# Peer memory of a two-block transformer on one core: score and output stages joined into one, coefficient table laid over the ranking and score buffers, keys turned behind score block 104, half of each group's gates applied by ScalarE

## What is computed

```python
def peer_ffn(xn, w_q, keys1, keys2, u_tab, v_tab):
    ...
    s1 = jnp.einsum('thd,kd->thk', q[:, :, 0], keys1)
    s2 = jnp.einsum('thd,kd->thk', q[:, :, 1], keys2)
    v1, i1 = lax.top_k(s1, PEER_TOPK)
    v2, i2 = lax.top_k(s2, PEER_TOPK)
    cand = (v1[..., :, None] + v2[..., None, :]).reshape(T, PEER_HEADS, PEER_TOPK * PEER_TOPK)
    ...
    top, pos = lax.top_k(cand, PEER_TOPK)
    eidx = jnp.take_along_axis(cidx, pos, axis=-1)
    g = jax.nn.softmax(top.astype(jnp.float32), axis=-1).astype(xn.dtype)
    ...
        a = jax.nn.gelu(jnp.einsum('td,thkd->thk', xc, u_tab[ec]), approximate=False)
        return jnp.einsum('thk,thkd->td', gc * a, v_tab[ec])
```

## Time and profile before

| | |
|---|---|
| median of 3 runs | 3219.14 us (3217.85 to 3222.44) |
| the profiled execution's own time | 3222.66 us |
| span from its first to its last instruction | 3220.8 us |
| granted TensorE clock, mean | 0.936 |
| PE / DVE / ACT / POOL busy, share of the span | 86% / 46% / 15% / 23% |
| bytes moved by DMA | 693.93 MB, mean 215 GB/s |

### The profile page before, as it was taken

The page is one execution under the profiler, slowest core; times in us unless marked ns, Lnnn a source line. Parts: engine busy times, 40 slices in busy tenths (PEclk is TensorE's granted clock), DMA queues, the critical chain, the costliest instruction groups (busy, mean ns, idle before and its releaser), DMA issues. The chain is left out here.

```text
span 3220.8 us, 30219 instructions
## 1 busy us (share of the span) xinstructions
PE 2779.2 (86%) x10080; PEld 1558.2 (48%) x10080; DVE 1478.4 (46%) x3007; ACT 489.8 (15%) x1015; POOL 732.9 (23%) x652
## 2 busy tenths in 40 slices
PE   6997899999997599959889989998980678888877
PEld 3445534447443433314435578887870543333333
DVE  1226200104012222232047249888679977777762
ACT  2124100001101011131137121111110310000002
POOL 0000000000000022110000004554466046766740
PEclk8997998999999699979999999999995999999998
DMA  5100251340122699941300019999999069999992
GB/s 203 50 27 28 105 192 43 134 173 37 52 79 83 268 392 396 387 187 60 111 14 1 27 60 346 413 399 354 418 415 365 38 248 413 413 414 413 413 363 85
DMA packets 133341, 693.93 MB, mean 215 GB/s; under 512 B 19571, under 2 KB 20979, under 8 KB 105587
## 3 DMA queue, kind: packets, MB, share of 16 engines
q1 hardware_dynamic: 50644, 408.32, 32.0%
q0 software_dynamic: 81792, 281.07, 22.1%
q10 hardware_dynamic: 800, 3.15, 0.3%
HBM read 701.90 MB, written 48.23 MB: 233 GB/s over the span
## 5 line engine op out<-in xcount | busy, mean ns | idle before, releaser
L428 PE MATMUL ps<-hT,wring 128*128 128x256 f32 (+1 forms) x2576 | 763.0, 458 | 30.2 <-ACT pk_g L2250 14.9
L428 PEld LDWEIGHTS ps<-hT,wring 128*128 128x128 f32 x2576 | 491.3, 191 | 296.7 <-issue 252.7
L2469 PE MATMUL ps<-pm_v_rows,pm_weighted 128*128 128x512 f32 x1024 | 465.2, 604 | 62.6 <-DVE pm_weighted L2519 44.7
L2144 POOL DMA_INDIRECT pk_ring<-in_peer_u,pk_rows x256 | 304.0, 1187 | 765.3 <-DVEq L2358 538.9
L2286 DVE CUSTOM_DVE_ANT_0 pk_ring<-pk_ring,mem_x 128x1024 f32<-128x1024 f32 x256 | 309.3, 1223 | 100.6 <-DMA pk_ring<-in_peer_u,pk_rows 87.9
L2469 PEld LDWEIGHTS ps<-pm_v_rows,pm_weighted 128*128 128x128 f32 x1024 | 186.6, 190 | 340.5 <-issue 230.4
L2437 POOL DMA_INDIRECT hT<-in_peer_v,pm_idxs x192 | 258.4, 1346 | 206.3 <-PE ps L2457 107.8
L2525 DVE SCALAR_TENSOR_TENSOR h_tok<-hT,gates,h_tok 128x1024 f32<-128x1024 f32 x192 | 244.7, 1282 | 100.4 <-DMA hT<-in_peer_v,pm_idxs 81.9
L1417 POOL COPY ex_idx<-row_token 128x1 uint32 (+1 forms) x24 | 4.4, 183 | 1222.3 <-PEq L1549 1090.3
L960 PE MATMUL ps<-wring,hT 128*128 128x512 f32 (+1 forms) x544 | 213.9, 555 | 1.2 <-PEq L376 1.2
L1604 DVE TENSOR_SCALAR hT<-ps,gain,ada 128x128 f32<-128x128 f32 x192 | 63.4, 403 | 215.9 <-PE ps L1505 215.9
(11 more groups left out here) (422 smaller groups left out, 2943.9 us busy)
## 6 DMA issues: line engine op xcount, KB each, us to landing
ex_gu<-in_experts SPq DMA_DIRECT2D x32, 2048.0 KB
pm_v_rows<-in_peer_v SPq DMA_DIRECT2D x64, 1024.0 KB
ex_dn<-in_experts SPq DMA_DIRECT2D x48, 1024.0 KB
wring<-in_w_in SPq DMA_DIRECT2D x21, 2048.0 KB, 8.9
wring<-in_peer_uT SPq DMA_DIRECT2D x21, 2048.0 KB
wring<-in_experts SPq DMA_DIRECT2D x16, 2048.0 KB
ada_w<-in_w_ada SPq DMA_DIRECT2D x12, 2048.0 KB
pk_u<-in_peer_uT SPq DMA_DIRECT2D x11, 2048.0 KB
```

The costliest lines, as they stand in the source:

```text
L428: mm = env.nc.tensor.matmul(out, w[:, k, lo:hi], rhs(k), start=(k == 0), stop=(k == KD - 1))
L2144: nc.gpsimd.indirect_dma_start(ring[:, n % RING, :], None, dram["peer_u"], bass.IndirectOffsetOnAxis(ap=rows[:, n // SLOTS, n % SLOTS:n % ...
L2469: mm = nc.tensor.matmul(env.ps[:, OUT[n], :], W[q][:, j * DS + t * P:j * DS + (t + 1) * P], vr[j // 2][:, j % 2 * D + half * WBLK:j % 2 * ...
```

## The change

Both memory stages become one function and one block, `stage_memory`.

- The table `C` (128 KiB for each partition) is laid over everything that ranking and scores need; only `coef`, `gate`, `rows` and `iota` have space of their own. `C`'s first 19 groups lie over the ranking's buffers, later ones over the score blocks, the stores' buffers and `xg`, the last one over `keyT`. The ring of the gathers is `env.wring` (8 buffers), the query weights' place, so POOL waits for the queries first.
- Score blocks of `peer_uT` are loaded in pairs (1 MiB, UBUF = 4 buffers) where it was quads (2 MiB, 3 buffers); stores of scores are 256 KiB (GBUF = 4 buffers) where they were 512 KiB (2 buffers).
- The keys are turned behind score 104. The exponential of tile 3 stands behind score 104 too (it was 70).
- EARLY = 19 of the 32 groups are built while the last 24 scores and the last dots run: one round is one group, then `beside(n)` scores on PE (one or two) and some dots on DVE. The other 13 groups follow when all scores and dots are done.
- In each group DVE multiplies only the first four tokens of B with the gate, ACT the other four.
- One list of 512 gathers; those of `peer_v` follow those of `peer_u` directly. SP's block loads of `peer_v` wait for the last group's product, since `vr` lies over A and B. The output loop is written out instead of `Fori`.

```diff
-UBUF = 3
-TABLE = (8, 36, 66)
+UBUF = 4
+GBUF = 4
+TABLE = (8, 36, 66, 104)
+EARLY = 19
...
+def beside(n):
+    at = lambda k: TABLE[3] + (PK - TABLE[3]) * k // EARLY
+    return at(n), at(n + 1)
...
+    def one_hots(n):
+        if n < EARLY:
+            return [env.hT[:, :, lo + n % 2 * P:lo + (n % 2 + 1) * P] for lo in (S, 0)]
+        return [spare[:, (lo + n % 2) * D:(lo + n % 2 + 1) * D].rearrange("p (t a) -> p t a", a=PK) for lo in (0, 2)]
...
             @block.gpsimd
...
+                for n in range(2 * GT * SLOTS):
...
                     if n >= RING:
-                        pool.wait_ge(G.used, n - RING + 1)
+                        pool.wait_ge(used, n - RING + 1)
...
             @block.sync
...
+                for t in c_t[EARLY - 1]:
+                    product_done(env, sp, t)
+                for n in range(QUADS):
+                    if n >= 2:
+                        sp.wait_ge(out_done, QUAD * (n - 1))
+                    nc.sync.dma_start(W[n % 2], dram["g_dram"][n]).then_inc(w_got[n % 2], 16)
+                    if n == 0:
+                        for t in c_t[-1]:
+                            product_done(env, sp, t)
+                    for m in (2 * n, 2 * n + 1):
...
+                        nc.sync.dma_start(vr[m % 2], v_pairs[m]).then_inc(v_got[m % 2], 16)
...
             @block.tensor
...
+                def coefficients(n):
+                    A, B = one_hots(n)
+                    pe.wait_ge(ab_done, 3 * n + 3)
+                    for half, tl in enumerate(c_t[n]):
+                        if half:
+                            pe.wait_ge(b_done, n + 1)
+                        bank_ready(env, pe, tl)
+                        for j in range(4):
+                            mm = nc.tensor.matmul(env.ps[:, tl[0], j * PK:(j + 1) * PK], A[:, 4 * half + j, :],
+                                                  B[:, 4 * half + j, :], start=True, stop=True)
...
-                table(TABLE[1], PK)
+                scores(TABLE[1], TABLE[3])
                 pe.wait_ge(gate_s, NT)
...
+                for n in range(GROUPS):
+                    coefficients(n)
+                    if n < EARLY:
+                        scores(*beside(n))
...
             @block.scalar
...
+                def coefficients(n):
+                    B = one_hots(n)[1]
+                    act.wait_ge(ab_done, 3 * n + 1)
+                    for j in range(4, GRP):
+                        ins = nc.scalar.activation(B[:, j, :], B[:, j, :], ACT.Copy, scale=keyT[:, 2, n * GRP + j:n * GRP + j + 1])
+                    ins.then_inc(b_done, 1)
...
+                    for half, tl in enumerate(c_t[n]):
+                        product_done(env, act, tl)
...
-                table(TABLE[2], TABLE[2] + 4)
+                scores(TABLE[2], TABLE[3])
                 exponentials(3)
-                table(TABLE[2] + 4, PK)
...
             @block.vector
...
+                def one_hot(n):
+                    A, B = one_hots(n)
+                    ts = slice(n * GRP, (n + 1) * GRP)
+                    if n in (0, 1):
+                        for tl in key_t:
+                            evacuated(env, ve, tl)
+                    elif n == EARLY:
+                        product_done(env, ve, u_t[-1])
+                    else:
+                        product_done(env, ve, c_t[n - 2][1])
...
+                    V.tensor_tensor(B[:, 0:4, :], B[:, 0:4, :], keyT[:, 2, n * GRP:n * GRP + 4].unsqueeze(2).broadcast_to([P, 4, PK]),
+                                    ALU.mult).then_inc(ab_done, 1)
...
                 finish(NT - 1)
-                for _ in range(GT * SLOTS):
-                    dot()
+                done = dot() + 1
+                for n in range(EARLY):
+                    one_hot(n)
+                    upto = done + (GT * SLOTS - done) * (n + 1) // EARLY
+                    while done < upto:
+                        done = dot() + 1
+                for n in range(EARLY, GROUPS):
+                    one_hot(n)
...
+                for m in range(PK):
+                    n = m // QUAD
+                    if m % QUAD == 0:
+                        ve.wait_ge(w_got[n % 2], w0[n % 2] + 16 * (n // 2 + 1))
+                    here = W[n % 2][:, m % QUAD * DS:(m % QUAD + 1) * DS]
+                    V.tensor_tensor(here, here, C[:, :, m], ALU.mult).then_inc(w_done, 1)
...
```

More of the change, by code:

```diff
@@ new lines, in stage_memory @@
+    u_t += env.tiles(TABLE[3] - TABLE[1])
+    key_t, c_t = env.tiles(2), []
+    for n in range(GROUPS):
+        c_t.append(env.tiles(2))
+        if n < EARLY:
+            u_t += env.tiles(beside(n)[1] - beside(n)[0])
+    turns = list(env.turns)
+    OUT = [0, 1, 2, 3]
+    blks = [env.take_block(q_t[1][3]), env.take_block(q_t[1][7])]
+    u_in, u0 = zip(*(env.again(f"table_in{n}", 16 * PAIRS // UBUF) for n in range(UBUF)))
+    (w_got, w0), (v_got, v0) = (zip(*(env.again(f"table_in{n}", c) for n in ns)) for ns, c in (
+        ((0, 1), 16 * QUADS // 2), ((2, 3), 16 * PAIRS // 2)))
@@ new lines, in stage_memory @@
+    got, got0 = zip(*(env.again(f"gathered{r}", 16 * 2 * GT * SLOTS // RING) for r in range(RING)))
+    g_out = [env.sem(f"pm_g_out{n}") for n in range(GBUF)]
+    in_s, top_s, exp_s, rows_s, gate_s = (env.sem("pm_" + n) for n in ("in", "top", "exp", "rows", "gate"))
+    used, ab_done, b_done, act_s, coef_s, w_done, out_done, sum_s = (env.sem("pm_" + n) for n in (
+        "used", "onehot", "gated", "gelu", "coef", "weighted", "out", "sum"))
+    v_pairs = dram["peer_v"].rearrange("(a c b) d -> c a (b d)", c=PAIRS, b=2)
@@ new lines, in stage_memory @@
+    ring = [env.wring[:, r // 4, r % 4 * D:(r % 4 + 1) * D] for r in range(RING)]
+    spare = env.hT[:].rearrange("p k t -> p (k t)")
+    vr = [spare[:, n * 2 * D:(n + 1) * 2 * D] for n in range(2)]
+    W = [spare[:, (4 + n) * D:(5 + n) * D] for n in range(2)]
+    def one_hots(n):
+        if n < EARLY:
+            return [env.hT[:, :, lo + n % 2 * P:lo + (n % 2 + 1) * P] for lo in (S, 0)]
+        return [spare[:, (lo + n % 2) * D:(lo + n % 2 + 1) * D].rearrange("p (t a) -> p t a", a=PK) for lo in (0, 2)]
@@ new lines, in _ @@
+                for tl in c_t[-1]:
+                    evacuated(env, ve, tl)
+                for m in range(PK):
+                    n = m // QUAD
[3 more added lines that the diff above has]
+                    V.tensor_tensor(here, here, C[:, :, m], ALU.mult).then_inc(w_done, 1)
+                    for t in range(GT):
+                        k = GT * SLOTS + GT * m + t
+                        r = k % RING
+                        ve.wait_ge(got[r], got0[r] + 16 * (k // RING) + 16)
+                        ve.wait_ge(used, k - 1)
+                        V.scalar_tensor_tensor(env.h[:, t, :], ring[r], coef[:, t, m:m + 1], env.h[:, t, :],
+                                               ALU.mult, ALU.add).then_inc(used, 1)
@@ L2679, in second_block @@
     stage_norm(env, "ffn2", tok, [(0, NT, gain("g_ffn"), None)], env.hT)
-    G = env.picked
-    G.used = env.sem("mem_used")
-    G.got, G.got0 = zip(*(env.again(f"gathered{r}", 16 * 2 * GT * SLOTS // RING) for r in range(RING)))
-    with nc.sbuf_tensor("mem_x", [P, GT, D], F32) as xg:
-        stage_memory_scores(env, xg, G)
-    env.close_ring()
-    stage_memory_outputs(env, G)
-    env.open_ring()
+    stage_memory(env)
     stage_norm(env, "ple", tok, [(0, NT, gain("g_ple"), None)], env.hT)
```

374 lines of the change are left out of this document (137 added, 237 removed).

## The result

The changed kernel takes 3237.71 us (median of 5 runs, 3234.39 to 3243.07) against 3219.14 us: ratio 1.0056, 95% interval 1.0041 to 1.0071, so it is **slower by about 18 us**. The forecast was 3195 us.

The account below looks back on a forecast made before the run. Three stretches were taken as bound by bytes, the table by DVE with memory idle. Step times put T at 2578.3 instead of 2603.1 (-24.8); with +1 for `vr` and rounding, -24: 3195 us against 3219.14, range 3177 to 3215.

Parts of the forecast that it names:

- T: End of PE's last group, where the table is done and outputs start: 2603.1 us before, 2578.3 forecast.
- rounds 0 to 8: First nine table groups with 108 dots: 148.8 us of DVE work plus 3 of waits, ending at 2466.9.
- rounds 9 to 18: Next ten groups, only 7 dots and 13 scores: PE is the slower, last score ends at 2538.9.
- groups 19 to 31 and the end: After the last score: 13 groups at 2.85 us, 37.1 us on DVE, then PE's last product, 2.05 + 0.3.
- Score 104: Before the table: exponential behind score 104 ready at 2303.8, so DVE waits some 17 us at `finish(3)`.
- Keys turned: Before the first group: gates ready at 2311.2, then transposes and ACT's copies, taken as 4 us; start at 2315.
- the full ring: Gathers fill 8 buffers during DVE's wait before `finish(3)`; 10 us taken off the bytes' 155 to 158 us.
- The link through ACT: Rounds 9 to 18: ACT multiplies its four tokens only behind the previous score's evacuation; 0.2 us a round, 2 in all.
- outputs shorter: Rival for the output stretch: written-out code takes 516 us instead of 528, at most -12, giving 3184 us; chance 0.13.
- half clock: Rival: PE stays at half clock from round 9 on, costing 64 and 16 us more, giving 3275 us; chance 0.07.
- Waits build up: Rival: late keys, dots waiting for bytes (12 rather than 3 us), ACT late; +15, giving 3210 us; chance 0.17.
- Even spread: Dots spread evenly over 19 rounds of 10 us: T near 2550, time 3167; excluded by instruction order, no chance given.

Follow-up runs that it names:

- the long pause: Changed kernel plus a 128x128 memset on DVE behind each dot: 3220.12 us, ratio 0.9991; with the dots also shared out evenly: 3173.01 us, 0.9842.

## Why the prediction was wrong

T came at 2617.0 where 2578.3 was forecast. By the steps:

| step | forecast | measured | difference |
|---|---|---|---|
| first group starts | 2315 | 2308.8 | -6.2 |
| rounds 0 to 8 | 151.9 us | 189.1 | **+37.2** |
| rounds 9 to 18 | 72.0 | 77.9 | +5.9 |
| groups 19 to 31 and the end | 39.4 | 41.2 | +1.8 |

- *Score 104.* Right: the exponential was ready by 2300 and DVE waited 21.4 us (17 forecast) in `finish(3)`. Putting it earlier gained 9 us, less than half of the wait, since the keys' place is the next thing that is late.
- *Keys turned.* The exponential was ready 3.5 us earlier than forecast, and PE began at 2305.5, 5.7 us earlier than the forecast's 2311.2. ACT wasn't late this time: its copies ended at 2307.6. DVE came to the first group at 2308.8 straight from its dots and waited for nothing, hence the 6 us.
- *Rounds 0 to 8*, **the step that failed**: "DVE and DMA are nearly level, so some waits stay: +3, with 0 and 12 as bounds". DVE's work was near the sum (189.1 - 34.9 = 154.2 us against 148.8). The waits for gathers were 34.9 us. I had taken a gather's rate from the bytes, and POOL's part of it as free. In its place the runs show that a gather waits on POOL for a boundary between DVE's operations: where DVE's dots stand back to back, gathers come every 2.29 us instead of 1.24. With a pause that only lengthens DVE's step, rounds 0 to 8 take 166.6 us, and with dots of one input 161.1. The first two rows hinted at it in the kernel before: POOL's busy time by its instructions is 1.27 us each over the ranking and 1.08 with the last dots. A smaller part is the 10 us taken off for the full ring. POOL issued 110 gathers in these rounds against 108 dots, so the ring was full again at their end and the bytes (62.9 MB) were nearly all there; without that, the forecast's 155 to 158 us for the bytes stand, and 157.4 was measured without most one-hots. So of the 37 us some 28 to 32 are held gathers (189.1 against 157.4 to 161.1), the rest fits the ring's 10 us, though no run tried it by itself.
- *Rounds 9 to 18.* Bound by PE, as forecast, at a clock of 0.95. The link through ACT was sized too small: 0.2 us a round forecast, and PE waited for ACT's four multiplications nine times, up to 0.8 us and 7.2 in all where 2 were forecast, its weight loads 8.9 (the waits from 2497.9 to 2575.8):

```profile
PEld ps L2271 <- ACT hT L2346: 8.9, 9, 1.0
...
PE ps L2271 <- ACT hT L2346: 7.2, 9, 0.8
```

- *Groups 19 to 31.* 2.87 us each at first and 3.00 later; right. *Outputs*: from 2700 to 2800 us they stand at 413 GB/s as in the earlier trace rows, and T to the end is 619.3 us against 617.7; right. The rival "outputs shorter" did not come.
- *The rivals.* The half clock did not come: 0.95 to 1.00 from round 9 on. It was 0.68 in the mean of rounds 0 to 8, where PE stood idle for 15 to 21 us in each of six rounds, and cost nothing there, since PE wasn't the bound. "Waits build up" named the right place, "dots waiting", but priced it at 12 us; it was 35.
- *Even spread*, named in the forecast as 3167 and not built: 3183 as it stands, and 3173 with the long pause.

So of the 43 us between forecast and median, 37 are one step. The uneven sharing of dots had been seen and counted, but it also made the miss dearer: rounds 1 to 6, with 11 to 17 dots each, are where back-to-back dots starve the ring, and rounds 9 to 18, with nearly none, can't give the time back. Evenly shared, the same slow gathers cost less: the long pause gains 10 us there (3183 to 3173) and 18 with the uneven rounds. They cost 26 us again once DVE has less of its own to do (3179 to 3154).

The Trainium skill, "SBUF — State Buffer", section "Who interferes with whom", has the rule: a DVE instruction with two SBUF inputs contends with a GpSimd instruction that reads SBUF, and the port pair that they share is an exclusive lock. The traces agree (gathers of 1.97 us beside dots, 0.94 beside sums), if the gather is taken as an instruction that reads its row numbers from SBUF; that reading is argued, no run here took the row numbers elsewhere. The section also reports a probe in which `tensor_tensor` didn't stall DMA; for these gathers the measurement differs (1.91 us beside such a product, above), and it decides. The page gives no time for a gather, so what the rule costs here comes from the rows alone.

## What to carry to other kernels

Before work is put beside gathers issued by GpSimd, look at how long one gather takes in the trace and what DVE runs at that moment: here operations with two SBUF inputs, back to back, nearly halved the rate of gathers though both engines looked less than full. Where their period was just short of the gather's, a small operation that lengthened it to the gather's period made the kernel faster. And a share-out that is recomputed from what is left runs out early; spread it from the fixed total if the other engine's work is even.

## What the runs showed of the hardware

- Beside back-to-back DVE operations of 1.145 us with two SBUF inputs, a gather's time on POOL goes from 0.94 to 1.99 us and gathers come every 2.29 us; with the operations 1.23 us apart, every 1.24 (0.94 each); beside sums of about 1.15 us with one input and a narrow output, back to back, every 1.24.
- A held gather ended 0.89 to 0.91 us behind the start of the DVE operation at which it was let go. The longest one shown was held through three operations, 3.49 us.
- An added 128x128 memset (0.17 us in the row) lengthened DVE's step by 0.08 us only, since it overlaps its neighbours; one of a single element by 0.02 us.
